# Key pages of decode attention in a decoder-layer kernel: the first two groups move out of the input projection into the last solver level

## The reference, cut to what matters

```python
k_past = cache_k[l][page_table].reshape(DB, past, DA_HEADS, 2, DA_QK)
...
lp = jnp.einsum('bqhmd,bkhmd->bhmqk', q, k_past, preferred_element_type=jnp.float32)
ln = jnp.einsum('bqhmd,bkhmd->bhmqk', q, k, preferred_element_type=jnp.float32)
logits = jnp.concatenate([lp, ln], axis=-1) * DA_SCALE
attn = _diff_weights(logits, lam).astype(v.dtype)
```

## Time and profile before

| | us |
|---|---|
| three timed runs | 1221.85 median (1220.05 to 1225.54) |
| the profiled execution, own time | 1217.92 |
| its span in the trace | 1216.1 |
| TensorE busy in the span | 1179.4 (97%) |
| VectorE / ScalarE / GpSimd busy | 819.9 / 512.2 / 90.2 |

### The profile page before, as it was taken

The page is one execution under the profiler, slowest core; times in us unless marked ns, Lnnn a source line. Parts: engine busy times, 40 slices in busy tenths (PEclk is TensorE's granted clock), DMA queues, the critical chain, the costliest instruction groups (busy, mean ns, idle before and its releaser), DMA issues.

```text
span 1216.1 us, 29018 instructions
## 1 busy us (share of the span) xinstructions
PE 1179.4 (97%) x12282; PEld 1064.7 (88%) x12282; DVE 819.9 (67%) x1155; ACT 512.2 (42%) x794; POOL 90.2 (7%) x89
## 2 busy tenths in 40 slices
PE   9999999999999999998989998999999999999996
PEld 8999999999999988886557445698999999999995
DVE  4875895699457554354665643787885797579754
ACT  5432442244334864434443434334742244244323
POOL 0000000000020210001450121020000000000021
PEclk9999999999999999999999999999999999999998
DMA  6223233233313667646665999641223222323211
GB/s 222 95 91 133 94 102 101 104 105 106 104 36 122 258 240 243 231 153 223 201 212 180 304 313 304 226 175 55 89 92 101 100 105 92 135 74 106 100 36 71
DMA packets 56722, 177.35 MB, mean 146 GB/s; under 512 B 7185, under 2 KB 7442, under 8 KB 47250
## 3 DMA queue, kind: packets, MB, share of 16 engines
q1 hardware_dynamic: 53426, 169.48, 40.8%
q10 hardware_dynamic: 3168, 6.02, 1.4%
HBM read 164.64 MB, written 10.83 MB: 144 GB/s over the span
## 4 chain that ended last, share of the span: by engine, by line
PE 86%; DVE 5%; SPq 4%; issue 2%; ACT 2%; DMA 1%; DVEq 0%; POOL 0%; POOLq 0%
PE banks L388 36%; PE banks L593 30%; PE banks L1296 3%; SPq L3153 2%; PE banks L2035 2%; PE banks L411 2%; PE banks L1043 2%; SPq L3145 1%; PE banks L2333 1%; PE banks L2105 1%; PE banks L908 1%; PE banks L3318 1%; PE banks L2408 1%; DVE weights_lo L367 1%; PE banks L2183 1%
## 5 line engine op out<-in xcount | busy, mean ns | idle before, releaser
L367 DVE TENSOR_TENSOR weights_lo<-weights_raw,weights_hi 128x1024 fp32r<-128x1024 f32 (+1 forms) x90 | 106.8, 1196 | 98.5 <-ACT weights_hi L359 97.9
L359 ACT ACTIVATE weights_hi<-weights_raw 128x1024 fp32r<-128x1024 f32 (+1 forms) x90 | 90.8, 1018 | 164.3 <-PE banks L388 144.3
L388 PE MATMUL banks<-hidden_hi,weights_hi 128*128 128x260 f32 x576 | 116.4, 283 | 0.0
L388 PE MATMUL banks<-hidden_hi,weights_lo 128*128 128x260 f32 x576 | 115.6, 282 | 0.0
L388 PE MATMUL banks<-hidden_lo,weights_hi 128*128 128x260 f32 x576 | 115.6, 282 | 0.0
L388 PE MATMUL banks<-x_hi,weights_hi 128*128 128x260 f32 x544 | 111.4, 286 | 0.0
L388 PE MATMUL banks<-x_hi,weights_lo 128*128 128x260 f32 x544 | 109.6, 283 | 0.0
L388 PE MATMUL banks<-x_lo,weights_hi 128*128 128x260 f32 x544 | 109.4, 283 | 0.0
L388 PEld LDWEIGHTS banks<-x_hi,weights_hi 128*128 128x128 f32 x544 | 83.7, 188 | 12.3 <-issue 11.7
L593 PE MATMUL banks<-x_sums_hi,more_weights_hi 128*128 128x260 f32 x320 | 90.6, 283 | 0.0
L593 PE MATMUL banks<-x_sums_hi,more_weights_lo 128*128 128x260 f32 x320 | 90.6, 283 | 0.0
(11 more groups left out here) (409 smaller groups left out, 3007.2 us busy)
## 6 DMA issues: line engine op xcount, KB each, us to landing
cache_pages<-in_cache_k SPq DMA_DIRECT2D x128, 256.0 KB, 3.6
weights_raw<-in_gate_up_b SPq DMA_DIRECT2D x22, 1024.0 KB, 4.8
weights_raw<-in_gate_up_a SPq DMA_DIRECT2D x21, 1024.0 KB, 4.8
cache_pages<-in_cache_v SPq DMA_DIRECT2D x56, 256.0 KB, 3.8
weights_raw<-in_w_in SPq DMA_DIRECT2D x13, 1024.0 KB, 5.5
projected<-in_cache_v SPq DMA_DIRECT2D x48, 256.0 KB, 3.8
weights_raw<-in_down_a SPq DMA_DIRECT2D x8, 896.0 KB, 4.6
weights_raw<-in_down_b SPq DMA_DIRECT2D x8, 896.0 KB, 4.6
```

Of the source, the lines that this page charges most:

```text
L359: nc.scalar.activation(WH[pr.slot(i, k)][:, 0:nk, :], RAW[slot][:, 0:nk, P * (k % 2):P * (k % 2) + P], ACT.Copy).then_inc(split_hi, 1)
L367: nc.vector.tensor_tensor(WL[pr.slot(i, k)][:, 0:nk, :], RAW[slot][:, 0:nk, P * (k % 2):P * (k % 2) + P], WH[pr.slot(i, k)][:, 0:nk, :].bi ...
L388: mm = nc.tensor.matmul(acc[s][:, a, 0:HALF], w[slot][:, t, :], x[:, k0 + t, HALF * a:HALF * a + HALF], start=begins and t == tiles[0] and ...
```

## The change

Key groups begin behind slab 12 rather than slab 10 (`FIRST_KEYS`), so the projection holds 14 of them, and `Groups` starts counting at 14. Two further groups stand in the last level of phase one, one behind each half level's turn, so that all 32 are again done at the end of the solve. ScalarE's copies of the quarters move with them: the first from slab 17 to slab 19, the second from behind slab 25 to the end of the opening, the third from behind level 2 to behind level 3. On SP the pages are shifted by one pair against the blocks of weights.

```diff
+        FIRST_KEYS = 12
...
-                if j >= 10:
-                    if j == 10:
+                if j >= FIRST_KEYS:
+                    if j == FIRST_KEYS:
                         pe.wait_ge(acc_free[3], inp.used0[3])
                         pe.wait_ge(g("consts_in"), 16)
                         pe.wait_ge(g("query_set"), 8)
-                    decode_keys_tensor(pe, j - 10)
+                    decode_keys_tensor(pe, j - FIRST_KEYS)
...
-                if j in (17, 25):
-                    decode_logits_scalar(act, j // 25)
+                if j == 19:
+                    decode_logits_scalar(act, 0)
...
-                self.n = N_IN - 10
+                self.n = N_IN - FIRST_KEYS
...
-        LEVEL_GROUPS = ((0, 0, 0, 0, 0, 0, 0, 0, 0, 0), (0, 1, 1, 1, 1, 1, 1, 1, 1, 1))
+        LEVEL_GROUPS = ((0, 0, 0, 0, 0, 0, 0, 0, 1, 1), (0, 1, 1, 1, 1, 1, 1, 1, 1, 1))
...
                 nc.scalar.activation(EPS[:, 5:6], EPS[:, 4:5], ACT.Exp)
+                decode_logits_scalar(act, 1)
...
-                if not a and l == 2:
+                if not a and l == 3:
                     decode_logits_scalar(act, 2)
...
                 input_block(n)
-                page_group(2 * n - 14)
-                page_group(2 * n - 13)
+                if n > 8:
+                    page_group(2 * n - 16)
+                    page_group(2 * n - 15)
...
-            for k in range(12, 18):
+            for k in range(10, 18):
                 page_group(k)
```

## The result

| | before | after |
|---|---|---|
| median of 16 timed runs each, same chip | 1222.72 us | 1228.43 us |
| lowest and highest | 1219.78, 1225.54 | 1223.94, 1232.45 |
| the profiled execution, own time | 1217.92 us | 1229.36 us |
| its span | 1216.1 us | 1227.6 us |

The ratio is 1.0047 with a 95% interval of 1.0035 to 1.0059: the changed kernel is 5.7 us slower (4.3 to 7.2). The forecast was +2.4 us and 1224.3; the time is also 0.4 us beyond the upper end of the range.

A forecast was written before the change was run, and what follows sets the result against it. TensorE, busy 97% of the span, was taken as the bound, with page arrival through a two-slot ring deciding the last level. Projection -2.33 us and last level +4.7 gave +2.4 on 1221.85: 1224.3 us, range 1219.0 to 1228.0.

The forecast's parts named there:

- keeps its neighbours: From slab 12 on: everything has the same work beside it and runs 2.33 us earlier.
- Projection, -2.33 us: Projection: two slabs without their key groups go from 6.93 to 5.77 us each, 2.33 us less in sum.
- ScalarE's copies at nothing: Three moved bank copies on ScalarE, 0.6 us each, were costed at nothing.
- Groups 24 and 25 without a wait: Last level: the first two of four key groups find their pages loaded and wait for nothing.
- The waits for pages: Last level: group 26 waits 2.7 us and group 27 1.8 us; the level becomes 4.7 us longer (3.8 to 5.7).
- The clock: Rival, last level: the granted clock falls once in the new gaps, costing 1.7 us; +4.1 us, 1226.0; chance 0.12.
- the rival of the long fall: Clock falls in the last level's gaps, stays at 1.2 GHz through the solve: up to 8 us more, 1232; chance 0.04.
- Neither made up nor grown: Behind the last level: the 4.7 us stay as they are, since all later work starts from events that move along.
- The sum: Whole kernel: -2.33 + 4.7 = +2.4 us (1.5 to 3.4).
- The base: Time the sum was added to: the timed runs' median of 1221.85 us, not the profiled execution's 1217.92.
- The page on DMA: Rule of fixed 2.0 us plus bytes at 436 GB/s: last loads of groups 26 and 27 there at 618.4 and 621.5.

The follow-up runs named there:

- g_half: The changed kernel with four tiny zero-adding matmuls (16 instructions) beside its key groups 1 and 2; 1230.92 us in one execution.
- experiment 5: The changed kernel with matmuls that add zero in the waits before groups 26 and 27; 1.0040 against the kernel before.
- g_early: e_early with eight tiny zero-adding matmuls beside key groups; 1.0006 against the kernel before.
- e_early: The changed kernel with its two extra groups behind the first product of levels 1 and 2, not in the last level; 1.0017 against the kernel before.

## Why the prediction was wrong, point by point

The difference from the kernel before is 3.3 us above the forecast of +2.4. Two steps failed, and the sum had nothing for either: that everything from slab 12 on "keeps its neighbours" (1.2 to 1.8 us were lost in levels 0 and 1), and that the clock stays at full behind the waits (1.3 us). The price of the waits themselves was right.

- **Projection, -2.33 us.** Right to 0.01 us in the trace. (The two slabs that became shorter are 11 and 12, each behind a group that is gone; and the stretch from 397 to 551 us holds the last 22 slabs, not 16. The sum is the same.) Wrong was the sentence that everything from slab 12 on "keeps its neighbours and runs 2.33 us earlier". The change moves TensorE's instructions to other places of its program, and with them the fetch of a block of code, which then meets the reload of the gates. Level 0 gives 2.1 us of the gain back in the first pair of traces; over levels 0 and 1 the three traces of before average 23.8 us and the two of after 25.6, and over all traces of either program it is 24.4 and 25.6. With eight tiny matmuls level 0 is back at 10.4 us, and the kernel is 2.8 us faster (0.1 to 5.5). This step failed, and no part of the sum held it.
- **ScalarE's copies at nothing.** No trace shows a wait behind them.
- **Groups 24 and 25 without a wait.** Right.
- **The waits for pages.** Place and sum right: group 27 starts 12.81 us behind PT, forecast 13.0 us, and its last page lands 12.8 to 13.7 us behind PT in the six traces with four groups of full pages in the level. In the kernel with the fetch put back, whose clock had recovered when it landed, the whole level is 15.37 us, which is 4.7 us longer than before, the forecast's number; with g_half's later pages it is 16.29 us, so the exact hit is in part luck. The division was off: 2.46 and 0.56 us, not 2.7 and 1.8, because slow work filled the second wait. From first issue to last landing group 27 took 5.5 us (forecast 6.2, between 5.3 and 7.2), but SP issued it 3.9 us behind group 26's, not 3.3 to 3.5; over all traces with four groups in the level it is 3.3 to 5.1 us.
- **The clock.** Given as a rival with 0.12, it came in both traces of after and in all others that keep four groups in the level, but for the one that fills the waits. It costs 1.4 us from group 27 to PT in the first trace, 1.3 us by the comparison in experiment 5. At half the clock a group took 1.94 us instead of 1.06 and Z 1.14 instead of 0.69, so less than the doubling that the rival of the long fall had. It should have been part of the forecast: the prediction read the earlier trace rows as a fall behind a level short of work, and itself put 4.5 us of waits into this one.
- **Behind the keys.** "Neither made up nor grown" holds for the solve (18.98 against 19.00 us). In phase two about 2 us seem to be lost; their cause is open.
- **The sum.** By the traces of the two kernels: -2.3, +1.8 in levels 0 and 1, +5.9 to 6.3 in the last level, together +5.4 to +5.8; the timed runs say +5.7 (4.3 to 7.2). That this agrees to a tenth is luck: with all traces levels 0 and 1 give +1.2, and phase two another +2.1, together +6.9 to +7.3. With the fetch put back: -2.2 (the tiny matmuls take about 0.2), -0.5 to +0.3 for levels 0 and 1 (23.23 us against before's mean, or against its two short traces), +4.7, which is +2.0 to +2.8; the runs say +2.9 (0.7 to 5.1). The forecast was +2.4.
- **The base.** The median of the three runs shown, 1221.85, was 0.9 us below that of 16 runs. Set on the longer series, the forecast's own sum would have been at 1225.1.
- **The page on DMA.** The Trainium skill's page "DMA: Bandwidth & Descriptors" (section "Anatomy of one DMA", measured on the GpSimd path) has the fit that gave an estimate of 2.6 us for 256 KB. By it the last loads of groups 26 and 27 would have landed at 618.4 and 621.5, in the times of before. The trace of after has 620.5 and 624.5, and its last level runs 1.2 us later: 619.3 and 623.3, where the forecast had 619.6 and 623.5. The measurement decides: beside three other loads the slowest load of a group took 3.8 and 3.9 us here, not 2.6.

## What to carry to other kernels

A gap in an engine's time is not room for work that needs data: count how fast the ring behind it can turn (here a group of pages each 3.3 us at best, and about 5 us or more from its first issue to its last landing), over the whole stretch that the ring serves, and then add what the new wait does to the clock. Where an edit makes a program longer or shorter ahead of a tight place, code can be fetched at another moment; if a stage gets slower without any change of its own, look at the queue of kind "instruction" beside the DMA that it waits for. And take a base and its stage lengths from more than one trace: here the one I had was 5 us below the usual.

## What the hardware showed unexpectedly

- One packet of 16 KB of code, at 1 to 2 us, goes with a transfer of 260 KB that lands in 4.7 to 5.5 us instead of 2.9 to 3.3 (nine traces against three), and a stage of 10 us becomes 2 us longer. That the fetch is the cause is supported by eight matmuls that only shift it: they bring a short level 0 back in both orders that were tried, with one trace each, and half of them, which did not shift it, did not. The timed runs are 2.8 us (0.1 to 5.5) and 1.4 us faster, the second within the noise. Why the transfer loses 2 us to so short a packet, and why readings between -0.5 and +0.5 us scatter from 3.7 to 5.3, is open.
- The wait of ScalarE for that reload and the length of the clock's fall behind it go together. In four of the five traces with a reload under 4 us the clock fell for 3.4 us, and in the fifth (g_early) not at all; in eleven of the twelve with a longer one it fell for 6.8 us, and in e_early's for 3.4.
- A group of four loads with a quarter of the bytes still needs 3.6 to 4.9 us.
